# First shift and scale summed on TensorE in four column blocks, beside two open projection chunks

## What is computed

```python
mod = jax.nn.silu(c) @ ada_w[l] + ada_b[l]           # c: (1, 1024), ada_w: (1024, 6144)
sh_m, sc_m, g_m, sh_f, sc_f, g_f = jnp.split(mod, 6, axis=-1)
h = modulate(rms_norm(x, mix_norm_w[l]), sh_m, sc_m) # xn * (1 + scale) + shift
proj = h @ w_in[l]                                   # w_in: (1024, 3336)
y_r = rwkv7_group(proj[..., :RWKV_COLS], ...)
y_m = mlstm_group(proj[..., RWKV_COLS:], ...)
```

## Time and profile before

| what | value |
|---|---|
| device time, median of three runs | 1258.65 us (1250.43 to 1260.34) |
| device time of the profiled execution | 1263.12 us |
| its span | 1261.0 us |
| mean granted TensorE clock | 0.914 |
| PE matmul busy | 85% of the span |
| DVE, ACT, POOL busy | 51%, 28%, 14% |
| DMA | 287.48 MB, 228 GB/s over the span |

### The profile page before, as it was taken

How to read it: one execution, slowest core, us unless ns; L and a number is a source line. 1 busy time by engine, 2 the same in 40 slices (tenths; PEclk the granted TensorE clock), 3 DMA queues, 4 the chain that set the end, 5 groups by cost and what they waited for, 6 DMA issues and landing times.

```text
span 1261.0 us, 16196 instructions
## 1 busy us (share of the span) xinstructions
PE 1074.6 (85%) x6588; PEld 817.6 (65%) x6588; DVE 638.4 (51%) x812; ACT 351.5 (28%) x440; POOL 170.9 (14%) x224
## 2 busy tenths in 40 slices
PE   1699987999978889989639795979999976999994
PEld 1578853997535555555218674858888865888883
DVE  4556658546444323323046727375757467553433
ACT  0122014341111111111023104165445215543530
POOL 5400113000100133321020004011111130000000
PEclk9999967999977999999769896779999977999998
DMA  9897728204679999998979603057676461545510
GB/s 344 245 303 252 263 93 332 102 1 168 221 283 409 402 401 356 363 351 319 409 250 369 249 3 131 1 180 264 224 294 237 134 241 76 187 147 195 221 67 34
DMA packets 117162, 287.48 MB, mean 228 GB/s; under 512 B 19398, under 2 KB 45278, under 8 KB 117098
## 3 DMA queue, kind: packets, MB, share of 16 engines
q1 hardware_dynamic: 94514, 245.45, 52.1%
q10 hardware_dynamic: 11032, 27.33, 6.3%
q0 software_dynamic: 11552, 13.79, 3.6%
HBM read 334.23 MB, written 2.62 MB: 267 GB/s over the span
## 4 chain that ended last, share of the span: by engine, by line
PE 67%; DMA 14%; DVE 10%; SPq 3%; ACT 2%; ACTq 2%; issue 2%; POOL 1%; DVEq 0%; POOLq 0%
PE ps L573 29%; DMA arena<-in_moe_w_down_dram 6%; PE ps L2249 4%; PE ps L2584 4%; PE ps L2563 4%; PE ps L2423 3%; DMA ring<-in_w_in_dram 3%; DMA macc<-in_ada_w_dram 3%; PE ps L2611 3%; PE ps L2251 2%; PE ps L2510 2%; PE ps L2689 2%; SPq L763 1%; PE ps L1210 1%; SPq L619 1%
## 5 line engine op out<-in xcount | busy, mean ns | idle before, releaser
L578 DVE TENSOR_TENSOR ring_parts<-ring,arena_parts 128x2048 fp32r<-128x2048 f32 x65 | 146.6, 2285 | 49.8 <-ACT arena_parts L1098 43.2
L573 PE MATMUL ps<-arena_parts,macc_parts 128*128 128x512 f32 x512 | 165.9, 396 | 0.0
L573 PE MATMUL ps<-arena_parts,gate_parts 128*128 128x512 f32 x288 | 115.4, 401 | 8.0 <-DVE hT_parts L578 8.0
L573 PE MATMUL ps<-ring_parts,gate_parts 128*128 128x512 f32 x288 | 114.3, 397 | 0.0
L573 PE MATMUL ps<-arena_parts,hT_parts 128*128 128x512 f32 x288 | 114.2, 397 | 0.0
L573 PEld LDWEIGHTS ps<-arena_parts,macc_parts 128*128 128x128 f32 x512 | 96.2, 188 | 19.5
L573 PE MATMUL ps<-ring_parts,macc_parts 128*128 128x512 f32 x256 | 99.8, 390 | 0.0
L1098 ACT CAST arena_parts<-ring 128x2048 fp32r<-128x2048 f32 x32 | 60.4, 1908 | 86.2 <-DMA ring<-in_mlp_w_dram 44.1
L573 PEld LDWEIGHTS ps<-arena_parts,gate_parts 128*128 128x128 f32 x288 | 55.6, 193 | 20.3 <-DVE hT_parts L578 8.8
L2249 PE MATMUL ps<-hT,ring 128*128 128x256 f32 x288 | 68.0, 400 | 0.0
L2584 PE MATMUL ps<-ring,hT 128*32 128x256 f32 x1024 | 61.6, 394 | 4.2 <-DMA ring<-in_moe_w_gate_dram 2.7
(11 more groups left out here) (529 smaller groups left out, 1826.0 us busy)
## 6 DMA issues: line engine op xcount, KB each, us to landing
ring<-in_mlp_w_dram SPq DMA_DIRECT2D x40, 1024.0 KB, 7.6
arena<-in_moe_w_down_dram SPq DMA_DIRECT2D x16, 2048.0 KB, 12.3
ring<-in_ada_w_dram SPq DMA_DIRECT2D x29, 1024.0 KB, 9.0
ring<-in_mlp_w_dram ACTq DMA_DIRECT2D x24, 1024.0 KB, 7.1
ring<-in_moe_w_up_dram SPq DMA_DIRECT2D x10, 2048.0 KB, 18.5
ring<-in_moe_w_gate_dram SPq DMA_DIRECT2D x10, 2048.0 KB, 16.2
arena<-in_ada_w_dram SPq DMA_DIRECT2D x15, 1024.0 KB, 7.0
ring<-in_w_in_dram SPq DMA_DIRECT2D x13, 1024.0 KB, 12.3
```

What stands on the lines that cost most here:

```text
L573: ins = nc.tensor.matmul(o, l, r, start=start and i == 0, stop=stop and i == 2, skip_group_check=True)
L578: return eng.tensor_tensor(lo, x, hi.bitcast(F32), ALU.subtract)
```

## The change

The first two vectors no longer go through `ada_slot`. Their 8 MB come in eight loads `mix_part(j)` of 256 columns each (block b = j // 2, shift or scale = j % 2), in pieces of 1 KB. For each block PE multiplies them with `c1_b` (the entries of `c`, each repeated over 32 columns), four k tiles side by side in four groups of 32 columns ("rows": 16 matmuls); ACT copies the result (`mix_row`); PE sums the groups and turns them to columns ("cols": 4 matmuls); DVE adds bias and norm weight for two k tiles, and DVE and ACT apply them to one k tile of `hT` each, which was copied out of PSUM before. Then PE does these two k tiles of chunks 7 and 8 (`win_part`), which stay open over all four blocks. Chunks 9 and 10 follow whole.

Also: `w_in` and the norm now split the 1024 channels as (t p) instead of (p t). All DMA issues leave ACT's beginning: the small loads go to POOL, behind the norm's power. The small matmul and the `bias_rows` write move behind "w.if". Chunks 11 and 12 come ahead of "m.bc", chunk 0 takes the place of 11, chunks 1 and 2 that of 12 and 0. In `stream` the four early chunks stand first, and the ada chunks follow win 11. `ada_slot(9)` moves behind "m.rows" on DVE.

```diff
+        win_early = win_order[:4]
+        stream = [("win", n) for n in win_early]
+        for n, adas in ((11, (8,)), (12, (9, 10)), (0, (11, 12)), (1, (13, 14)), (2, (15, 16)), (3, (17,)), (4, (18,)),
+                        (5, (19,)), (6, (20, 21, 22, 23))):
+            stream += [("win", n)] + [("ada", i) for i in adas]
...
+            def mix_part(j):
+                b, vec = j // 2, j % 2
+                if j >= 4:
+                    sp.wait_ge(t["n"], STEP[f"n.rows{b - 2}"])
+                src = A["ada_w"][0].rearrange("(p t) n -> p t n", t=8)[:, :, vec * D + 256 * b:vec * D + 256 * b + 256]
+                sp.dma_start(mix_home[j % 4], src).then_inc(mix_in[j % 4], 16)
...
-            act.wait_ge(t_bias, 1)
-            nc.scalar.copy(ebc, ps[0:SWA_H, 4, 0:384]).then_inc(a_bias, 1)
-            act.wait_ge(a_bias, 1)
-            act.dma_start(scratch_d.rearrange("h (q l) -> h q l", q=P), ebc.unsqueeze(1).to_broadcast([SWA_H, P, 384])
-                          ).then_inc(bias_out, 16)
             act.wait_ge(x_in, 16)
-            a_norm(act, "n", mod_c[:, 0, :], mod_c[:, 1, :])
+            c = Counter(act, a["n"])
+            for tt in range(TT):
+                a_square(c, "n", tt)
...
+            for b in range(4):
+                act.wait_ge(t["n"], STEP[f"n.rows{b}"])
+                c.link(nc.scalar.copy(mix_row, ps[:, 4, :]))
+                c.at(f"n.row{b}")
+                act.wait_ge(v["n"], STEP[f"n.mod{b}"])
+                c.link(nc.scalar.activation(hT[:, 2 * b, :], hT[:, 2 * b, :], ACT.Identity,
+                                            bias=mod_c[:, 0, 2 * b:2 * b + 1], scale=mod_c[:, 1, 2 * b:2 * b + 1]))
...
+            def mix_rows(b):
+                if b:
+                    pe.wait_ge(a["n"], STEP[f"n.row{b - 1}"])
+                for vec in range(2):
+                    j = 2 * b + vec
+                    pe.wait_ge(mix_in[j % 4], 16 * (j // 4 + 1))
+                    for k in range(KT):
+                        quad = slice(32 * (k % 4), 32 * (k % 4) + 32)
+                        ins = nc.tensor.matmul(ps[quad, 4, 256 * vec:256 * vec + 256], c1_b[:, k, :], mix_home[j % 4][:, k, :],
+                                               start=k < 4, stop=k >= 4, skip_group_check=True)
+                n_.mark(ins)
+                n_.at(f"n.rows{b}")
+                pe.wait_ge(a["n"], STEP[f"n.row{b}"])
+                pe.wait_ge(v["n"], STEP["n.mixc"] if b == 0 else STEP[f"n.mod{b - 1}"])
+                for i in range(4):
+                    ins = nc.tensor.matmul(ps[:, 5, 64 + i:65 + i], mix_row[:, P * i:P * i + P], quad_one, start=True, stop=True)
...
+            for b in range(4):
+                mix_rows(b)
+                for n in win_early[:2]:
+                    win_part(n, (2 * b, 2 * b + 1))
...
+            for n in win_early[2:]:
+                win_part(n, range(KT))
...
+            pe.wait_ge(hot_in, 32)
+            nc.tensor.matmul(ps[0:SWA_H, 4, 0:384], rel_sb[0:33, :], hots[0:33, :], start=True, stop=True).then_inc(t_bias, 1)
```

More of the change, by code:

```diff
@@ L266, in program @@
         w_slot = small[:, 60:62]
+        quad_one = small[:, 62:63]
+        c1_b = macc[:, 1, 0:256].rearrange("p (k n) -> p k n", k=8)
+        mix_row = macc[:, 1, 256:768]
+        mix_home = [area(kb, SLOT).rearrange("p (t n) -> p t n", t=8) for kb in (0, 66, 22, 78)]
         third_gu = (0, 8, 40, 16)
@@ L1319, in _ @@
             cm.at("m.lf")
-            columns(9)
+            act.wait_ge(t_bias, 1)
+            nc.scalar.copy(ebc, ps[0:SWA_H, 4, 0:384]).then_inc(a_bias, 1)
+            act.wait_ge(a_bias, 1)
+            act.dma_start(scratch_d.rearrange("h (q l) -> h q l", q=P), ebc.unsqueeze(1).to_broadcast([SWA_H, P, 384])
+                          ).then_inc(bias_out, 16)
+            columns(11)
             act.wait_ge(v["m"], STEP["m.conv"])
@@ L1606, in _ @@
-            v_norm(dve, "n", mod_c[:, 0, :], mod_c[:, 1, :], mod_mix, meanwhile=lambda: ada_slot(6))
+            c.link(nc.vector.tensor_copy(c1_b, ccol[:, 0:8].unsqueeze(2).to_broadcast([P, 8, 32])))
+            dve.wait_ge(g["c"], STEP["c.ident"])
+            c.link(nc.vector.tensor_reduce(quad_one, ident[:, 0:P:32], AX_X, ALU.add))
+            c = Counter(dve, v["n"])
+            for tt in range(TT):
+                v_mean(dve, c, "n", tt)
+            for tt in range(TT):
+                v_xn(dve, c, "n", tt)
@@ new lines, in _ @@
+            for b in (0, 2):
+                dve.wait_ge(t["n"], b + 1)
+                c.link(nc.vector.tensor_copy(hT[:, 2 * b:2 * b + 2, :], ps[:, b, :].rearrange("p (k t) -> p k t", k=2)))
+                c.at(f"n.ev{b}")
+            dve.wait_ge(t["n"], STEP["n.mix"])
+            c.link(nc.vector.tensor_copy(mix_c[:, :], ps[:, 5, 0:24]))
+            c.at("n.mixc")
+            for b in range(4):
+                dve.wait_ge(t["n"], STEP[f"n.cols{b}"])
+                shift, scale = mod_c[:, 0, 2 * b:2 * b + 2], mod_c[:, 1, 2 * b:2 * b + 2]
+                c.link(nc.vector.tensor_tensor(shift, ps[:, 5, 64:66], mix_c[:, 2 * b:2 * b + 2], ALU.add))
+                c.link(nc.vector.tensor_tensor(scale, ps[:, 5, 66:68], mix_c[:, 8 + 2 * b:10 + 2 * b], ALU.add))
+                c.link(nc.vector.scalar_tensor_tensor(scale, scale, 1.0, mix_c[:, 16 + 2 * b:18 + 2 * b], ALU.add, ALU.mult))
+                c.at(f"n.mod{b}")
+                k = 2 * b + 1
+                c.link(nc.vector.tensor_scalar(hT[:, k, :], hT[:, k, :], mod_c[:, 1, k:k + 1], mod_c[:, 0, k:k + 1],
+                                               ALU.mult, ALU.add))
+                c.at(f"n.v{b}")
@@ L1649, in _ @@
             cm.at("m.rows")
+            ada_slot(9)
             ada_slot(10)
@@ L2232, in _ @@
[L2232 to L2238 removed]
+            for tt in range(TT):
+                pe.wait_ge(v["n"], STEP[f"n.xn{tt}"])
+                for k in range(KT):
+                    o = (k % 2) * 256 + tt * P
+                    ins = nc.tensor.transpose(ps[:, k // 2, o:o + P], xn[:, tt, P * k:P * k + P], ident[:, :])
+                    if tt == 1 and k % 2:
+                        n_.mark(ins)
@@ new lines, in win_part @@
+            def win_part(n, ks):
+                loaded(pe, ("win", n))
+                pe.wait_ge(a["n"], STEP[f"n.a{ks[-1] // 2}"])
+                pe.wait_ge(v["n"], STEP[f"n.v{ks[-1] // 2}"])
+                w = slot(("win", n)).rearrange("p (t n) -> p t n", t=8)
+                for j in range(2):
+                    o = win_bank(n)[:, 256 * j:256 * j + 256]
+                    for k in ks:
+                        l, r = ((w[:, k, P * j:P * j + P], hT[:, k, :]) if n < 9 else (hT[:, k, P * j:P * j + P], w[:, k, :]))
+                        ins = nc.tensor.matmul(o, l, r, start=j == 0 and k == 0, stop=k == KT - 1, skip_group_check=True)
+                if ks[-1] == KT - 1:
+                    ins.then_inc(t_win, 1)
@@ new lines, in _ @@
+            for b in range(4):
+                mix_rows(b)
+                for n in win_early[:2]:
+                    win_part(n, (2 * b, 2 * b + 1))
+                if b == 1:
+                    pe.wait_ge(prm_in, 16 * 14)
+                    nc.tensor.transpose(ps[:, 0, 256:312], prm[0:56, :], ident[0:56, 0:56])
+                    c.mark(nc.tensor.transpose(ps[:, 0, 312:408], prm2[0:96, :], ident[0:96, 0:96]))
+                    c.at("w.prm")
+            for n in win_early[2:]:
+                win_part(n, range(KT))
@@ L2258, in scores @@
                                         start=True, stop=True)
-            for n in (7, 8):
-                columns(n)
             pe.wait_ge(gate_in, 16 * 7)
@@ L2283, in _ @@
             m.at("m.sc0")
-            columns(11)
+            columns(0)
             pe.wait_ge(v["m"], STEP["m.z"])
@@ L2302, in _ @@
             m.at("m.num")
-            for n in range(1, 6):
+            for n in range(3, 6):
                 columns(n)
```

143 lines of the change are left out of this document (70 added, 73 removed), and 7 rows, old and new, of the table STEP.

## The result

The changed kernel takes 1264.48 us (median of 20 runs, 1256.55 to 1274.10), the kernel before 1258.40 in as many runs of the same session. The ratio is 1.0073, with a 95% interval of 1.0049 to 1.0097: 9.2 us slower, 6 to 12 by the interval. The forecast was 1262.3 us, +3.6. So the change does not pay, as said, and it costs 2.5 (by the medians) to 5.6 us more than said.

What follows compares the result with a forecast made beforehand. PE was taken to bound the kernel almost without a gap from 70.9 us, after a late `w_in` load. Block chain -6.0 and write +9.6 gave +3.6 on 1258.65: 1262.3 us, range 1250 to 1271.

Steps and rivals of the forecast that it cites:

- The block chain: PE's work from the start through the four blocks up to T: T at 79 us, 6.0 us earlier than 84.97.
- T: Time when chunks 7 to 10, w.if and the bias matmul are done on PE: 79 us, against 84.97 before.
- the thin part: In each block, ACT's copy, cols, DVE's small steps, applying and hand-overs: 4.1 us, 1.9 of it cols.
- the dense part: In each block, 16 instructions of chunks 7 and 8, then the next rows: 6.65 us in all.
- The clock: PE's clock falls in each block and comes back 4.2 us into the dense part: 13 instructions slow, 3 fast.
- Rival B: PE's clock stays low through the blocks: T = 87.7, wait +12.4, 1271.1 us; chance 0.12.
- Rival D: PE's clock stays high in the blocks and win 2 is late: -13.3 + 9.6 = -3.7, 1255.0 us; chance 0.08.
- The loads keep up: Block loads and win 7 to 10 all land in time, with 2 us to spare in block 1, more later.
- The write: Moved `bias_rows` write on eight engines delays win 2: PE waits 7.6 us plus 2 of slow clock, cost 9.6.
- from T + 8 the slow engines pass 146 packets until the write ends: Loads share the slow engines with the write until T + 39.4; win 2 lands at T + 41.5.
- Rival A: Behind chunk 11 the write hides and win 2 is in time: 1252.7 us, 1245.4 with clock high; chance 0.23.
- The shift carried unchanged: The shift at ACT's copy of chunk 6 (the copy, 170.7 us before) stays the same to the end: +3.6 us.

Runs made afterwards that it cites:

- The extra matmuls: Changed kernel with spread write, plus matmuls nobody reads ahead of the transposes and in the block gaps; ratio 0.9933 to the kernel before.
- the mean of three: Kernel before, unchanged, profiled three times: ACT's copy of chunk 6 at 170.72, 166.46 and 169.99 us, mean 169.06.
- the version with the small loads later: Changed kernel with spread write and extra matmuls, POOL's small loads held until the second block's rows are done; ratio 0.9895 to the kernel before.
- the two others: Changed kernel with spread write and extra matmuls, with those ahead of the transposes (ratio 0.9933 to before) or in block gaps only (0.9968).

## Why the prediction was right, and where it was not

**The block chain.** Right: T = 78.85 against 79, gain 6.1 against 6.0. Not each term was: the thin part is 3.3 us and not 4.1, since the cols take 1.05 and not 1.9 (0.13 us an instruction, where the row of 32 in the earlier trace rows gave 0.235, though it too began at a granted clock of 1.00; what makes that row slower was not looked into), while the dense part with the next rows takes 7.3 against 6.65, and 8.7 in the first block. The two errors cancel (-3.3 and +3.3 us over the four blocks), and that T is met to 0.2 us is luck to that extent.

**The clock.** Right in the mechanism: it falls in each block, at the start of the dense part or just behind it, and is back near its end. Rival B, the clock low throughout with T at 87.7, is out. The extra matmuls priced it: 1.7 us a block (5.38 against 3.69) and 3.0 in the first. Rival D, the clock high by itself, put T at 71.7. With the clock held high T was 75.22, since the loads bind, and 71.35 with POOL's small loads out of their way. "The loads keep up" held in the first profile of the changed kernel; in the second the rows of the third block waited 0.98 us for a load, and with the clock high the loads bind.

**The write.** Right in the cause: it lies on half of the engines, takes 0.216 us a packet there (the earlier trace rows had 0.21), and is issued where two late loads stand behind it. It ran for 32 us, as forecast. The step that failed is "from T + 8 the slow engines pass 146 packets until the write ends": it let q1 share from the first packet. They pass almost nothing of q1 until about 64 of the write's packets each are through. Both windows of the earlier trace rows lie over 20 us behind the write's issue at 31.8 us, where by the pace of 33 packets a us the first 64 of each engine are out, and their packets of q1 are those of all 16 engines: they could not show it. So win 1, given as landed by T + 22, landed at T + 37.6, with the write's end, and PE wanted it at T + 26.7. The wait is on win 1 and not on win 2. The term was 9.6 (7.6 and 2 of a cold clock) and measured 12.8 (10.9 and 1.9). That the two are so near is partly luck: a wait on another load, for another reason, ends near the write's end too. The prediction also had win 2 issued right behind ada 14; SP was held there until T + 22. Rival A, that the write hides, is out: -6.0 at the copy needed a write of another shape.

**The shift carried unchanged.** +6.4 us at the copy against the one profile of before, +8.1 against the mean of three, +9.2 timed. With that mean the step holds within what the repeats differ by. What the prediction lacked is that the mark of before itself moves by 4 us from run to run, 3 of them by the clock in chunks 11 and 6, so that a sum made against one profile carries an error as large as the change. And the 3.6 us of the forecast stand against 6.1 by the medians and 9.2 by the ratio: at the copy the term of the write adds 3.2 and the wait at the column sums 0.7, the shorter cold part of chunk 6 takes 1.4 back, and the rest can't be told from this scatter. The last sentence of the forecast, that a difference which grows behind 175 us would prove it wrong, was too strict: in the first profile it grew by 5.0 us, in the second it shrank by 1.8.

## What to carry to other kernels

A DMA from a few partitions costs others more than its bytes: it can fill its engines for tens of us, and a load behind it landed only about when it ended. Before such a write is moved next to loads with little slack, spread its source over all partitions; here that turned a change of +0.7% into one that can't be told from none (-0.06%, interval -0.35% to +0.22%), and with the gaps of PE filled and the small loads held back it became -1.05%. Before a sum is made against one profile, see how far its marks move in a second one.

## What the runs showed of the hardware that was not expected

- 1.5 KB packets out of partitions 0 to 7 or 0 to 15 take 0.216 us each on their engine, out of 8 partitions spaced 16 apart 0.124, out of all 128 0.081.
- While an engine works off the first 64 or so packets of one queue, the other queue gets next to nothing on it: 11 packets of q1 in 5 us, and none from 85 to 99 us when the write lay on all engines. It is not a fixed time: with packets that cost little over half, q1 came in again 9 us behind the write's first packet and not 15.
- The issue of a load behind such a write takes long itself: 8.1 us on SP, and 0.4 where the write, spread, had landed.
- The write's own pace does not suffer from the loads: 165 packets in 5 us while q1 moved 11, 162 while it moved 627.
- With small matmuls in the gaps of 0.8 and 1.5 us the granted clock stayed at 1.00 through all four blocks of the version with the small loads later, over waits of 0.94 and 1.83 us; in the two others it fell once, behind waits of 0.89 and 3.27 us and of 1.16 and 2.17 us.
- One kernel's clock falls at different places from run to run: chunk 11 of the kernel before took 8.79, 7.10 and 8.13 us in three profiles, chunk 6 10.12, 8.74 and 9.77.
